# First conditioning in blocks of 512 columns, with a second ring of slots, in a diffusion backbone's inference step

## Chip, cores and metric

The kernel runs on one core of a Trainium2 chip. The metric is the device time of one execution in microseconds (us); it is lower when better. Engines are named as the profile names them: PE is TensorE (matmuls; PEld its weight loads), DVE is VectorE, ACT is ScalarE, POOL is GpSimd, SP is SyncE, which here only issues transfers.

## What is computed

Two layers of a backbone work on 128 context tokens and 256 latent tokens, 2048 wide. The part that matters is the start of a layer: the conditioning vectors (one for each of the two token groups) go through silu and the matrix w_ada, which gives six vectors; the first two, shift and scale, modulate the normalised tokens before the input projection.

```python
mods = jnp.split(jax.nn.silu(cvec) @ lp['w_ada'] + lp['b_ada'], 6, axis=-1)
sh1, sc1, g1, sh2, sc2, g2 = [m[:, None, :] for m in mods]
h = rms_norm(x, lp['g_pre1']) * (1.0 + sc1) + sh1
z = h @ lp['w_in']
...
x = x + g1 * rms_norm(mix, lp['g_post1'])
h = rms_norm(x, lp['g_pre2']) * (1.0 + sc2) + sh2
f = jnp.square(jax.nn.relu(h @ lp['w_mlp1'])) @ lp['w_mlp2']
x = x + g2 * rms_norm(f, lp['g_post2'])
```

w_ada is 2048 x 12288 per layer, in 32-bit floats. Nothing else of the layer can start before shift and scale of layer 0 are there: their 4096 columns (32 MB of weights) are the "first conditioning".

## The kernel before

Each engine has its own instruction stream, and semaphores order them. The first stage of layer 0, up to about 157 us, does four things beside each other.

Loads (SP, L371 to L376). SP first loads the conditioning vectors and x, and then, for each of eight pairs i, the weights of two blocks of 256 columns: block i (shift) and block 8 + i (scale). A block is four units of 512 rows x 256 columns, 512 KB each (`load_ada`, L342). The units go round a ring of four slots, `ada_raw`: SP waits on `ada_used` until the slot's last unit has been used by PE. Behind each pair comes one load of w_in (256 rows x 512 columns, `load_wide`, L335) into the ring `raw`, also of four slots. SP issues strictly in this order, so a waiting load holds back all loads behind it.

Conditioning (PE, `ada_unit`, L1462; `ada_turn`, L1473). For a unit PE does four matmuls of 256 columns with 32 columns of stationary data, each into its own quarter of the partitions of a bank of PSUM. When a block's four units are done, DVE copies the sums out (`ada_copy`, L829), PE turns and adds the quarters with two small matmuls, and DVE adds the bias and writes `mods` (`ada_mods`, L833). In PE's stream the turn of a block stands behind the second unit of the next block.

Rows (DVE, `first_rows`, L999; ACT, `h_high`, L563). With a pair's shift and scale the tiles 2i and 2i + 1 of the normalised, transposed x (in `full`) are modulated: DVE computes the coefficients, scales four pieces, ACT rounds the result to `h_hi`, and DVE subtracts for `h_lo`. Between the two DVE does `w_low` for a unit of w_in; ACT does `w_high` for it.

Projection (PE, `unit_rows`, L1535). The first four tiles of columns of the input projection are accumulated in banks 0 to 3 as rows become ready: one row unit is 24 matmuls of 384 columns, in four quarters of six. PE's order is written out by hand (L1547 to L1562): the quarters of row unit n/2 - 2 stand behind the units of even blocks n from 4 on; row units 6 and 7 stand after the last turn. x is turned into `full` (L1526) after the first three blocks; ACT counts the copies in `x_copied`. Afterwards ACT copies the four tiles to `z` (L558), and the next stage begins.

The memory of `z` is not in use in this stage but for `facc`, which holds x before it is turned.

Of the kernel before, what the change touches and what calls it, by code (L numbers as in the profile page):

```python
# [31 lines left out]
F32 = mybir.dt.float32  # L32
F32R = mybir.dt.float32r
ALU = mybir.AluOpType
# [3 lines left out]
P = 128  # L38
D = 2048
DEPTH = 2  # L40
CTX, LAT = 128, 256
TOK = CTX + LAT
# [71 lines left out]
PAIRS = 8  # L114
MOD = 256
# [47 lines left out]
def backbone(nc, x_prompt, x_sample, cache_k, cache_v, c, c_ctx, w_ada, b_ada, g_pre1, g_post1, g_pre2,  # L163
# [3 lines left out]
    with ctx:  # L167
        def sem(name):
            return ctx.enter_context(nc.semaphore(name))
# [7 lines left out]
        def at(name, shape, dt, offset):  # L177
            return nc.alloc_sbuf_tensor_at(name, [P, *shape], dt, offset=base + offset)
# [76 lines left out]
        junk = at("junk", [2, NC], F32, z_at + 4 * 16 * TOK)  # L255
        stats_at = z_at + 4 * (19 * TOK + 256)
# [19 lines left out]
        ada_landed = [sem(f"ada_landed{s}") for s in range(SLOTS)]  # L276
        hi_ready, lo_ready, unit_used, acc_free = sems("hi_ready lo_ready unit_used acc_free")
# [50 lines left out]
        def _(sp):  # L328
# [13 lines left out]
            def load_ada(layer, m, j, wait=True, n=None):  # L342

                n = m if n is None else n
                if wait:
                    sp.wait_ge(ada_used, 4 * n + j - 3)
                src = w_ada[layer, 512 * j:512 * j + 512, bass.ds(m * UC, UC)]
                sp.dma_start(ada_raw[:, j, :, :], src.rearrange("(k p) n -> p k n", p=P)).then_inc(ada_landed[j], 16)
# [467 lines left out]
        def _(dve):  # L816
# [12 lines left out]
            def ada_copy(n, bank=BANK_ADA):  # L829
                dve.wait_ge(ada_used, 4 * n + 4)  # L830
                nc.vector.tensor_copy(ada_s[:, :], ps[:, bank, 0:UC]).then_inc(ada_copied, 1)

            def ada_mods(layer, m, n, bank=BANK_ADA):  # L833
                dve.wait_ge(ada_turned, n + 1)
                nc.vector.tensor_tensor(mods[:, layer, bass.ds(m * 2, 2), :],
                                        ps[:, bank, MOD:MOD + 4].rearrange("p (t g) -> p t g", g=2),
                                        pb[:, layer, bass.ds(m * 2, 2)].unsqueeze(2).to_broadcast([P, 2, 2]),
                                        ALU.add).then_inc(mods_ready, 1)
# [160 lines left out]
            def first_rows(i):  # L999

                kts = slice(2 * i, 2 * i + 2)
                if i == 0:
                    dve.wait_ge(x_copied, 12)
                dve.wait_ge(mods_ready, 2 * i + 2)
                chain.link(nc.vector.scalar_tensor_tensor(
                    out=coef[:, 0, kts, :], in0=mods[:, 0, SC1 + 2 * i:SC1 + 2 * i + 2, :], scalar=1.0,
                    in1=pa[:, 0, G_PRE1 + 2 * i:G_PRE1 + 2 * i + 2].unsqueeze(2).to_broadcast([P, 2, 2]), op0=ALU.add, op1=ALU.mult))
                for kt in (2 * i, 2 * i + 1):
# [3 lines left out]
                last.then_inc(full_ready, 1)  # L1012
                w_low(i % 4, i // 4)
                dve.wait_ge(h_hi_ready, i + 1)
                nc.vector.tensor_tensor(h_lo[:, kts, :], full[:, kts, :], h_hi[:, kts, :].bitcast(F32),
                                        ALU.subtract).then_inc(h_ready, 1)

            for i in range(PAIRS):
                ada_copy(2 * i, ADA_FIRST[0])
                ada_mods(0, i, 2 * i, ADA_FIRST[0])  # L1020
                if i:
                    first_rows(i - 1)
                ada_copy(2 * i + 1, ADA_FIRST[1])
                ada_mods(0, PAIRS + i, 2 * i + 1, ADA_FIRST[1])
            first_rows(PAIRS - 1)

            for layer in range(DEPTH):
# [227 lines left out]
                def ada_products(lo, i, b, j, mark0):  # L1255
# [3 lines left out]
                    dve.wait_ge(ada_landed[j], 16 * (n + 1))  # L1259
# [104 lines left out]
        def _(pe):  # L1364
# [97 lines left out]
            def ada_unit(n, j, bank=BANK_ADA, read=None):  # L1462

                read = n if read is None else read
                pe.wait_ge(ada_landed[j], 16 * (n + 1))
                if j == 0 and not (isinstance(read, int) and read <= 0):
                    pe.wait_ge(mods_ready, read)
                for g in range(4):
                    last = nc.tensor.matmul(ps[32 * g:32 * g + 32, bank, 0:UC], cond[:, 4 * j + g, :], ada_raw[:, j, g, :],  # L1469
                                            start=j == 0, stop=j == 3)  # L1470
                last.then_inc(ada_used, 1)

            def ada_turn(n, bank=BANK_ADA, read=None):  # L1473

                read = n if read is None else read
                pe.wait_ge(ada_copied, n + 1)
                if not (isinstance(read, int) and read <= 0):
                    pe.wait_ge(mods_ready, read)
                for t in range(2):
                    last = nc.tensor.matmul(ps[:, bank, MOD + 2 * t:MOD + 2 * t + 2], ada_s[:, P * t:P * t + P], sel[:, :],  # L1480
                                            start=True, stop=True)
                last.then_inc(ada_turned, 1)

# [63 lines left out]
            for n in range(2 * PAIRS):  # L1547
                for j in range(4):
                    ada_unit(n, j, ADA_FIRST[n % 2], n - 1)
                    if j == 1 and n:  # L1550
                        ada_turn(n - 1, ADA_FIRST[(n - 1) % 2], n - 2)
                    if n >= 4 and n % 2 == 0:
                        unit_rows(n // 2 - 2, j)
                if n == 0:
                    turn_rows()
                if n < 3:
                    for g in range(4 * n, 4 * n + 4):
                        turn_first_x(g)
            ada_turn(2 * PAIRS - 1, ADA_FIRST[1], 2 * PAIRS - 2)
# [264 lines left out]
```

## Time and profile before

| what | us |
|---|---|
| median of 3 runs | 3325.29 |
| lowest, highest run | 3323.32, 3329.78 |
| the profiled execution | 3325.19 |
| its span, first to last instruction | 3323.4 |
| PE busy in the span | 3197.0 |
| DVE busy | 2178.8 |
| ACT busy | 1118.7 |
| end of the first stage, from the span's start | 156.9 |

The profile is of one execution. Busy time is summed per engine; matmuls are pipelined and their ends are modelled, so a busy PE need not be at its peak. The chain of waits follows the work that ended last back from releaser to releaser. A window gives busy times, the granted clock of TensorE (1.00 is 2.4 GHz, 0.50 is 1.2 GHz), the share of time of the 16 DMA engines, and what they moved.

### The profile page before, as it was taken

How to read it: one execution, taken by the hardware profiler on the slowest of the kernel's cores; microseconds unless marked ns; L12 is line 12 of the kernel's file. 1: busy time of each engine (PE TensorE's matmuls, PEld its weight loads, DVE VectorE, ACT ScalarE, POOL GpSimd, SP SyncE). 2: the span in 40 equal slices, each digit the busy share in tenths (PEclk: the TensorE clock that was granted, in tenths of full speed). 3: DMA queues.
4: the chain of work that ended last, by engine and by line, in shares of the span. 5: the costliest groups of instructions: out<-in, count | busy, mean ns of one | idle time of the engine just before them, and what ended most of it. 6: DMA issues, size and time to landing. Idle time of an engine off the chain costs nothing.

```text
span 3323.4 us, 48314 instructions
## 1 busy us (share of the span) xinstructions
PE 3197.0 (96%) x17401; PEld 2774.8 (83%) x17401; DVE 2178.8 (66%) x3132; ACT 1118.7 (34%) x1567; POOL 180.7 (5%) x211
## 2 busy tenths in 40 slices
PE   6899999999999999999998999999999999999999
PEld 3588755788998988989987996679899899898997
DVE  2357665598989889889896787667556463333335
ACT  2122333442333323323334334344233233332332
POOL 0001033000000000000000202300000000000000
PEclk8899999999999999999999999999999999999999
DMA  9866475266666676666662431125545444344342
GB/s 301 278 195 202 150 245 166 77 216 221 228 211 208 216 235 223 221 216 227 211 199 92 121 125 56 64 76 178 171 138 174 157 151 127 127 127 129 129 127 102
DMA packets 420022, 566.40 MB, mean 170 GB/s; under 512 B 17688, under 2 KB 276368, under 8 KB 419504
## 3 DMA queue, kind: packets, MB, share of 16 engines
q1 hardware_dynamic: 417600, 560.02, 52.3%
q0 software_dynamic: 1344, 4.33, 0.4%
q8 instruction: 76, 1.25, 0.2%
q14 instruction: 58, 0.48, 0.0%
q10 hardware_dynamic: 944, 0.32, 0.0%
HBM read 560.93 MB, written 3.67 MB: 170 GB/s over the span
## 4 chain that ended last, share of the span: by engine, by line
PE 85%; DVE 7%; issue 3%; ACT 3%; DMA 2%; SPq 0%; DVEq 0%; ACTq 0%
PE ps L1371 41%; PE ps L1379 34%; PE ps L1469 2%; DMA ada_raw<-in_w_ada_dram 2%; DVE ada_sums L1272 1%; PE ps L1542 1%; DVE w_lo L826 1%; PE ps L1653 1%; PE ps L1627 1%; DVE conv L1057 1%; PE ps L1641 1%; PE ps L1400 1%; ACT facc L584 1%; ACT w_hi L544 1%; PE ps L1614 1%
## 5 line engine op out<-in xcount | busy, mean ns | idle before, releaser
L826 DVE TENSOR_TENSOR w_lo<-raw,w_hi 128x1024 fp32r<-128x1024 f32 x672 | 825.9, 1233 | 767.3 <-ACT w_hi L544 741.3
L544 ACT ACTIVATE w_hi<-raw 128x1024 fp32r<-128x1024 f32 x672 | 710.8, 1058 | 1480.5 <-PE ps L1379 780.7
L1371 PE MATMUL ps<-h_hi,w_hi 128*128 128x384 f32 x2752 | 929.8, 338 | 8.0 <-DVE w_lo L826 7.0
L1371 PE MATMUL ps<-h_hi,w_lo 128*128 128x384 f32 x2752 | 923.1, 335 | 0.0
L1371 PE MATMUL ps<-h_lo,w_hi 128*128 128x384 f32 x2752 | 923.1, 335 | 0.0
L1379 PE MATMUL ps<-w_hi,hid_hi 128*128 128x512 f32 x1536 | 600.7, 391 | 2.6 <-DVE facc L1292 2.6
L1379 PE MATMUL ps<-w_hi,hid_lo 128*128 128x512 f32 x1536 | 598.1, 389 | 0.0
L1379 PE MATMUL ps<-w_lo,hid_hi 128*128 128x512 f32 x1536 | 598.1, 389 | 0.0
L1272 DVE SCALAR_TENSOR_TENSOR ada_sums<-ada_raw,cond,ada_sums 128x512 f32<-128x512 f32 x840 | 575.3, 746 | 0.0
L1371 PEld LDWEIGHTS ps<-h_hi,w_hi 128*128 128x128 f32 x2752 | 519.1, 189 | 25.0 <-issue 11.5
L1371 PEld LDWEIGHTS ps<-h_lo,w_hi 128*128 128x128 f32 x2752 | 519.2, 189 | 1.1
L1371 PEld LDWEIGHTS ps<-h_hi,w_lo 128*128 128x128 f32 x2752 | 519.2, 189 | 0.0
L1379 PEld LDWEIGHTS ps<-w_hi,hid_hi 128*128 128x128 f32 x1536 | 288.3, 188 | 64.4 <-DVE facc L1292 5.5
L1379 PEld LDWEIGHTS ps<-w_lo,hid_hi 128*128 128x128 f32 x1536 | 288.3, 188 | 60.2
L1379 PEld LDWEIGHTS ps<-w_hi,hid_lo 128*128 128x128 f32 x1536 | 288.3, 188 | 58.9
L1379 PE MATMUL ps<-w_hi,h_hi 128*128 128x512 f32 x384 | 162.6, 423 | 0.0
L1379 PE MATMUL ps<-w_lo,h_hi 128*128 128x512 f32 x384 | 151.6, 395 | 0.0
L1379 PE MATMUL ps<-w_hi,h_lo 128*128 128x512 f32 x384 | 151.5, 395 | 0.0
L1469 PE MATMUL ps<-ada_raw,cond 128*32 128x256 f32 x1280 | 105.9, 417 | 46.1 <-DMA ada_raw<-in_w_ada_dram 39.3
L1057 DVE SCALAR_TENSOR_TENSOR conv<-glu,pc,conv 128x384 f32<-128x384 f32 x240 | 141.9, 653 | 0.0
L1292 DVE TENSOR_TENSOR facc<-facc,ps 128x512 f32<-128x512 f32 x168 | 115.1, 685 | 30.4 <-PE ps L1379 28.5
L781 ACT ACTIVATE z<-ps 128x768 f32<-128x768 f32 x64 | 52.2, 815 | 202.8 <-PE ps L1371 202.8
(192 smaller groups left out, 2054.9 us busy)
## 6 DMA issues: line engine op xcount, KB each, us to landing
raw<-in_w_mlp_dram SPq DMA_DIRECT2D x512, 512.0 KB, 4.0
ada_raw<-in_w_ada_dram SPq DMA_DIRECT2D x384, 512.0 KB, 4.6
raw<-in_w_in_dram SPq DMA_DIRECT2D x96, 512.0 KB, 4.6
raw<-in_w_out_dram SPq DMA_DIRECT2D x64, 512.0 KB, 3.6
out_dram<-x SPq DMA_DIRECT2D x6, 512.0 KB, 2.6
x<-in_x_sample_dram SPq DMA_DIRECT2D x1, 2048.0 KB, 10.3
pw_w<-in_w_conv_pw_dram POOLq DMA_DIRECT2D x2, 1024.0 KB, 8.3
x<-in_x_prompt_dram SPq DMA_DIRECT2D x1, 1024.0 KB, 5.0
```

The source lines that it names most:

```text
L544: nc.scalar.activation(w_hi[:, j % 4, :, :], raw[:, j % 4, :, :], ACT.Copy).then_inc(hi_ready, 1)
L584: nc.scalar.activation(facc[:, place(n), t, :], x[:, t, NC * n:NC * n + NC], ACT.Square, accum_out=ss_x[:, t, n:n + 1]).then_inc(x_squared, 1)
L781: nc.scalar.activation(z[:, 16:18, :], ps[:, 2 * pair:2 * pair + 2, 0:TOK], ACT.Relu).then_inc(acc_free, 1)
L826: nc.vector.tensor_tensor(w_lo[:, j % 4, :, :], raw[:, j % 4, :, :], w_hi[:, j % 4, :, :].bitcast(F32), ALU.subtract).then_inc(lo_ready, 1)
L1057: op = nc.vector.scalar_tensor_tensor(out=out, in0=src, scalar=w, in1=out, op0=ALU.mult, op1=ALU.add)
L1272: op = nc.vector.scalar_tensor_tensor(out=out, in0=src, scalar=by, in1=out, op0=ALU.mult, op1=ALU.add)
L1292: nc.vector.tensor_tensor(dst, dst, ps[:, BANK_ACC + t, :], ALU.add).then_inc(acc_added, 1)
L1371: last = nc.tensor.matmul(ps[:, 2 * pair + t, 0:TOK], w[:, j % 4, k, P * t:P * t + P], v[:, kt + k, :], start=begin and k == 0 and i == 0, ...
L1379: last = nc.tensor.matmul(ps[:, BANK_ACC + t, :], v[:, kt + k, tokens(t)], wide(w, j)[:, k, :], start=begin and k == 0 and i == 0, stop=en ...
L1400: last = nc.tensor.matmul(ps[:, 2 * (n % 2) + g, P * i:P * i + P], coef[:, k, 4 * n + i, g:g + 1].to_broadcast([P, P]), ident[:, :], start ...
L1469: last = nc.tensor.matmul(ps[32 * g:32 * g + 32, bank, 0:UC], cond[:, 4 * j + g, :], ada_raw[:, j, g, :], start=j == 0, stop=j == 3)
L1542: last = nc.tensor.matmul(ps[:, t, 0:TOK], wide(w, u)[:, k, P * t:P * t + P], v[:, 2 * u + k, :], start=u == 0 and k == 0 and i == 0, stop ...
```

## The change

The sixteen blocks of 256 columns of the first conditioning become eight blocks of 512 columns, in the order shift, scale, shift, scale and so on; a block is eight units of 256 rows x 512 columns (still 512 KB). A unit is two matmuls of 512 columns; even units go into the first two quarters of the partitions, odd ones into the last two. Units 4 to 7 of the blocks from 2 on go to a second ring of four slots, `ada_aside`, which lies in the memory of `z` where `facc` was; before its first load SP waits for the last copy of x. A block's sums are copied in two halves to `ada_row`, turned with four small matmuls and added in two halves. `first_rows` works on four tiles at once, with `w_low` of its first unit ahead of the wait for the scale. A load of w_in follows the fourth unit of each block. Row units start with block 3; row unit 5 stands around the last turn, 6 and 7 behind it.

```diff
+ADA_FIRST_BLOCKS = 8
+ADA_ASIDE = ADA_FIRST_BLOCKS - 2
...
+        ada_aside = at("ada_aside", [SLOTS, 4, UC], F32, z_at)
+        ada_row = at("ada_row", [NC], F32, z_at + 4 * 20 * TOK)
...
-            for i in range(PAIRS):
-                for h, m in enumerate((i, PAIRS + i)):
-                    for j in range(4):
-                        load_ada(0, m, j, wait=2 * i + h > 0, n=2 * i + h)
-                load_wide(i % 4, i // 4, w_in, 0, 2 * P * i, CA0 * P, wait=i >= 4)
+            for n in range(ADA_FIRST_BLOCKS):
+                for u in range(8):
+                    aside = n >= 2 and u >= 4
+                    if n <= 2 and not aside:
+                        if 8 * n + u >= 4:
+                            sp.wait_ge(ada_used, 8 * n + u - 3)
+                    elif n == 2:
+                        sp.wait_ge(x_copied, 12)
+                    else:
+                        sp.wait_ge(ada_used, 8 * (n - 1) + u + 1)
+                    col = D * (n % 2) + NC * (n // 2)
+                    src = w_ada[0, 2 * P * u:2 * P * u + 2 * P, col:col + NC].rearrange("(k p) n -> p k n", p=P)
+                    sp.dma_start(wide(ada_aside if aside else ada_raw, u), src).then_inc((aside_landed if aside else ada_landed)[u % 4], 16)
+                    if u == 3:
+                        load_wide(n % 4, n // 4, w_in, 0, 2 * P * n, CA0 * P, wait=n >= 4)
...
+            def rows_copy(n):
+                dve.wait_ge(ada_used, 8 * n + 8)
+                for b in range(2):
+                    nc.vector.tensor_copy(ada_row[:, UC * b:UC * b + UC],
+                                          ps[:, ADA_FIRST[n % 2], UC * b:UC * b + UC]).then_inc(ada_copied, 1)
+            def rows_mods(n):
+                tile = DT * (n % 2) + 4 * (n // 2)
+                dve.wait_ge(ada_turned, 2 * n + 2)
+                for b in range(2):
+                    kts = slice(tile + 2 * b, tile + 2 * b + 2)
+                    nc.vector.tensor_tensor(mods[:, 0, kts, :],
+                                            ps[:, ADA_FIRST[n % 2], 4 * b:4 * b + 4].rearrange("p (t g) -> p t g", g=2),
+                                            pb[:, 0, kts].unsqueeze(2).to_broadcast([P, 2, 2]), ALU.add).then_inc(mods_ready, 1)
+            def first_rows(c):
+                quad_kts = slice(4 * c, 4 * c + 4)
+                if c == 0:
                     dve.wait_ge(x_copied, 12)
+                w_low(2 * c % 4, c // 2)
+                dve.wait_ge(mods_ready, 4 * c + 4)
...
+                for kt in range(4 * c, 4 * c + 4):
                     for g, a, b in GROUPS:
                         last = nc.vector.tensor_scalar(full[:, kt, a:b], full[:, kt, a:b], coef[:, 0, kt, g:g + 1],
                                                        mods[:, 0, SH1 + kt, g:g + 1], ALU.mult, ALU.add)
+                    if kt % 2:
+                        last.then_inc(full_ready, 1)
+                for i in (2 * c, 2 * c + 1):
+                    kts = slice(2 * i, 2 * i + 2)
+                    if i % 2:
+                        w_low(i % 4, i // 4)
+                    dve.wait_ge(h_hi_ready, i + 1)
+                    nc.vector.tensor_tensor(h_lo[:, kts, :], full[:, kts, :], h_hi[:, kts, :].bitcast(F32),
+                                            ALU.subtract).then_inc(h_ready, 1)
+            for n in range(ADA_FIRST_BLOCKS):
+                rows_copy(n)
+                rows_mods(n)
+                if n % 2:
+                    first_rows(n // 2)
...
+            def rows_unit(n, u):
+                if n >= 2 and u >= 4:
+                    pe.wait_ge(aside_landed[u % 4], 16 * (n - 1))
+                else:
+                    pe.wait_ge(ada_landed[u % 4], 16 * (2 * n + u // 4 + 1 if n < 2 else n + 3))
+                if n >= 2 and u == 0:
+                    pe.wait_ge(mods_ready, 2 * (n - 1))
+                for k in range(2):
+                    g = 2 * (u % 2) + k
+                    last = nc.tensor.matmul(ps[32 * g:32 * g + 32, ADA_FIRST[n % 2], :], cond[:, 2 * u + k, :],
+                                            wide(ada_aside if n >= 2 and u >= 4 else ada_raw, u)[:, k, :], start=u < 2, stop=u >= 6)
+                last.then_inc(ada_used, 1)
+            def rows_turn(n):
+                for b in range(2):
+                    pe.wait_ge(ada_copied, 2 * n + 2)
+                    for t in (2 * b, 2 * b + 1):
+                        last = nc.tensor.matmul(ps[:, ADA_FIRST[n % 2], 2 * t:2 * t + 2], ada_row[:, P * t:P * t + P], sel[:, :],
+                                                start=True, stop=True)
+                    last.then_inc(ada_turned, 1)
...
+            for n in range(ADA_FIRST_BLOCKS):
+                for u in range(8):
+                    rows_unit(n, u)
+                    if u == 1 and n:
+                        rows_turn(n - 1)
+                    if n >= 3 and u % 2 == 0:
+                        unit_rows(n - 3, u // 2)
+                    if u % 4 == 3 and 2 * n + u // 4 < 3:
+                        if n == 0 and u == 3:
+                            turn_rows()
+                        for g in range(4 * (2 * n + u // 4), 4 * (2 * n + u // 4) + 4):
+                            turn_first_x(g)
+            unit_rows(ADA_FIRST_BLOCKS - 3, 0)
+            unit_rows(ADA_FIRST_BLOCKS - 3, 1)
+            rows_turn(ADA_FIRST_BLOCKS - 1)
+            unit_rows(ADA_FIRST_BLOCKS - 3, 2)
+            unit_rows(ADA_FIRST_BLOCKS - 3, 3)
             for u in range(PAIRS - 2, PAIRS):
                 for part in range(4):
                     unit_rows(u, part)
```

Lines of the old forms of these functions, and the counts of loads in later waits (less six, which went to the other ring), are left out.

## Rows read from the trace of the kernel before

**Rows 1.** The page's first part: busy us, share of the span, instructions.

```profile
PE 3197.0 (96%) x17401; PEld 2774.8 (83%) x17401; DVE 2178.8 (66%) x3132; ACT 1118.7 (34%) x1567; POOL 180.7 (5%) x211
```

**Rows 2.** Chain of waits, 0 to 260 us: shares by line; pieces (start, us, what).

```profile
by line: PE ps L1371 22.4%; DMA ada_raw<-in_w_ada_dram 22.3%; PE ps L1542 18.2%; PE ps L1469 13.5%; DMA raw<-in_w_in_dram 5.3%; DVE conv L1057 3.5%; DVE w_lo L826 3.4%; PE ps L1480 3.0%; PE ps L1532 2.4%; ACT w_hi L544 1.2%; SPq L348 1.1%; 
...
54.67 6.01 DMA ada_raw<-in_w_ada_dram
...
123.08 6.29 DMA ada_raw<-in_w_ada_dram
```

**Rows 3.** Waits, 44 to 140 us: who waited for whom, us, times, longest.

```profile
SPq L348 <- PE ps L1469: 75.1, 39, 4.1
...
PE ps L1469 <- DMA ada_raw<-in_w_ada_dram: 23.0, 11, 3.4
```

**Rows 4.** Windows: us, each engine's busy time (instructions), granted clock, DMA share, GB/s.

```profile
0.00:20.00 20.00, 3.44 (x25) 0.81 (x25) 2.39 (x12) 8.68 (x10) 2.27 (x13) 1.00 0.89 305
20.00:44.00 24.00, 19.42 (x174) 12.06 (x170) 8.16 (x24) 8.80 (x15) 0.00 (x0) 0.93 0.95 316
...
60.00:140.00 80.00, 62.55 (x459) 37.20 (x460) 18.21 (x46) 7.96 (x9) 0.00 (x0) 0.77 0.86 275
...
62.00:64.00 2.00, 2.00 (x10) 1.56 (x12) 0.00 (x0) 0.00 (x0) 0.00 (x0) 0.50 1.09 365
...
82.00:88.00 6.00, 6.00 (x45) 3.60 (x44) 0.59 (x2) 0.00 (x0) 0.00 (x0) 0.91 0.67 215
...
146.00:151.00 5.00, 5.00 (x16) 5.00 (x17) 4.63 (x9) 3.65 (x4) 1.13 (x2) 0.50 1.10 353
...
896.00:904.00 8.00, 8.00 (x37) 6.62 (x36) 4.41 (x7) 2.12 (x2) 0.00 (x0) 1.00 1.05 394
```

**Rows 5.** PE's groups by shape, 53.9 to 54.95 us: busy us, mean ns, idle.

```profile
L1469 PE MATMUL ps<-ada_raw,cond 128*32 128x256 f32 x16 | 1.1, 385 | 0.0
```

**Rows 6.** Chain of waits, single pieces of PE: start, us, line, instructions.

```profile
25.71 1.00 PE ps L1469 x16
...
50.39 0.57 PE ps L1469 x8
50.96 1.25 PE ps L1542 x6
...
61.81 2.22 PE ps L1542 x6
64.03 1.01 PE ps L1469 x8
...
140.38 0.55 PE ps L1480 x4
```

**Rows 7.** Timeline, 0 to 160 us: start, us, engine, line, operation, tiles, count.

```profile
38.47 2.00 ACT L662 ACTIVATE full<-ps 128x512 f32<-128x512 f32 x3 [0.26 <-PE ps L1532]
...
41.31 1.07 PE L1469 MATMUL ps<-ada_raw,cond 128*32 128x256 f32 x16
...
142.60 0.64 PE L1469 MATMUL ps<-ada_raw,cond 128*32 128x256 f32 x8 [1.00 <-DMA ada_raw<-in_w_ada_dram]
...
146.31 1.25 DVE L1010 TENSOR_SCALAR full<-full,coef,mods 128x128 f32<-128x128 f32 x4
...
147.59 0.84 ACT L565 ACTIVATE h_hi<-full 128x768 fp32r<-128x768 f32 x1 [0.79 <-DVE full L1010]
```

**Rows 8.** Chain of waits, end of the first stage: start, us, line, instructions.

```profile
145.88 11.01 PE ps L1542 x48
156.91 0.82 ACT z L558
```

**Rows 9.** DVE's groups by line, 60 to 140 us: busy us, mean ns, idle.

```profile
L826 DVE TENSOR_TENSOR w_lo<-raw,w_hi 128x1024 fp32r<-128x1024 f32 x4 | 4.9, 1218 | 0.0
L1015 DVE TENSOR_TENSOR h_lo<-full,h_hi 128x768 fp32r<-128x768 f32 x4 | 3.8, 952 | 0.0
L831 DVE COPY ada_s<-ps 128x256 f32<-128x256 f32 x9 | 3.8, 422 | 18.7 <-PE ps L1469 18.7
```

More of the change, by code:

```diff
@@ L276, in backbone @@
         ada_landed = [sem(f"ada_landed{s}") for s in range(SLOTS)]
+        aside_landed = [sem(f"aside_landed{s}") for s in range(SLOTS)]
         hi_ready, lo_ready, unit_used, acc_free = sems("hi_ready lo_ready unit_used acc_free")
@@ L340, in load_wide, with load_ada @@
                 sp.dma_start(wide(raw, j), src).then_inc(raw_landed[j % 4], 16)
[L342 to L346, printed above, removed]
+            def load_ada(layer, m, j):
+                sp.wait_ge(ada_used, 4 * m + j - 3)
                 src = w_ada[layer, 512 * j:512 * j + 512, bass.ds(m * UC, UC)]
@@ L827, in w_low, with ada_copy, ada_mods @@
                                         ALU.subtract).then_inc(lo_ready, 1)
-            def ada_copy(n, bank=BANK_ADA):
+            def ada_copy(n):
                 dve.wait_ge(ada_used, 4 * n + 4)
-                nc.vector.tensor_copy(ada_s[:, :], ps[:, bank, 0:UC]).then_inc(ada_copied, 1)
-            def ada_mods(layer, m, n, bank=BANK_ADA):
+                nc.vector.tensor_copy(ada_s[:, :], ps[:, BANK_ADA, 0:UC]).then_inc(ada_copied, 1)
+            def ada_mods(layer, m, n):
                 dve.wait_ge(ada_turned, n + 1)
                 nc.vector.tensor_tensor(mods[:, layer, bass.ds(m * 2, 2), :],
-                                        ps[:, bank, MOD:MOD + 4].rearrange("p (t g) -> p t g", g=2),
+                                        ps[:, BANK_ADA, MOD:MOD + 4].rearrange("p (t g) -> p t g", g=2),
                                         pb[:, layer, bass.ds(m * 2, 2)].unsqueeze(2).to_broadcast([P, 2, 2]),
@@ L998, in _ @@
             chain.link(nc.vector.tensor_scalar(nsinks[:, :, :], sinks[:, :, :], -1.0, None, ALU.mult))
-            def first_rows(i):
-                kts = slice(2 * i, 2 * i + 2)
-                if i == 0:
+            def rows_copy(n):
[14 more added lines that the diff above has]
+                if c == 0:
                     dve.wait_ge(x_copied, 12)
-                dve.wait_ge(mods_ready, 2 * i + 2)
+                w_low(2 * c % 4, c // 2)
+                dve.wait_ge(mods_ready, 4 * c + 4)
                 chain.link(nc.vector.scalar_tensor_tensor(
-                    out=coef[:, 0, kts, :], in0=mods[:, 0, SC1 + 2 * i:SC1 + 2 * i + 2, :], scalar=1.0,
-                    in1=pa[:, 0, G_PRE1 + 2 * i:G_PRE1 + 2 * i + 2].unsqueeze(2).to_broadcast([P, 2, 2]), op0=ALU.add, op1=ALU.mult))
-                for kt in (2 * i, 2 * i + 1):
+                    out=coef[:, 0, quad_kts, :], in0=mods[:, 0, SC1 + 4 * c:SC1 + 4 * c + 4, :], scalar=1.0,
+                    in1=pa[:, 0, G_PRE1 + 4 * c:G_PRE1 + 4 * c + 4].unsqueeze(2).to_broadcast([P, 4, 2]), op0=ALU.add, op1=ALU.mult))
+                for kt in range(4 * c, 4 * c + 4):
                     for g, a, b in GROUPS:
@@ L1011, in first_rows @@
                                                        mods[:, 0, SH1 + kt, g:g + 1], ALU.mult, ALU.add)
[L1012 to L1025, printed above, removed]
+                    if kt % 2:
[12 more added lines that the diff above has]
+                    first_rows(n // 2)
             for layer in range(DEPTH):
@@ L1258, in ada_products @@
                     begin = b % 2 == 0 and j == 0
-                    dve.wait_ge(ada_landed[j], 16 * (n + 1))
+                    dve.wait_ge(ada_landed[j], 16 * (n + 1 - ADA_ASIDE))
                     if begin:
@@ L1460, in h_wait, with ada_unit @@
                 pe.wait_ge(norm_lo, 12 * (p - 1) + 8 + j + 1)
[L1462 to L1467, printed above, removed]
+            def ada_unit(n, j):
+                pe.wait_ge(ada_landed[j], 16 * (n + 1 - ADA_ASIDE))
+                if j == 0:
+                    pe.wait_ge(mods_ready, n)
@@ L1468, in ada_unit, with ada_turn @@
                 for g in range(4):
-                    last = nc.tensor.matmul(ps[32 * g:32 * g + 32, bank, 0:UC], cond[:, 4 * j + g, :], ada_raw[:, j, g, :],
+                    last = nc.tensor.matmul(ps[32 * g:32 * g + 32, BANK_ADA, 0:UC], cond[:, 4 * j + g, :], ada_raw[:, j, g, :],
                                             start=j == 0, stop=j == 3)
                 last.then_inc(ada_used, 1)
-            def ada_turn(n, bank=BANK_ADA, read=None):
-                read = n if read is None else read
+            def ada_turn(n):
@@ L1476, in ada_turn @@
                 pe.wait_ge(ada_copied, n + 1)
-                if not (isinstance(read, int) and read <= 0):
-                    pe.wait_ge(mods_ready, read)
+                pe.wait_ge(mods_ready, n)
                 for t in range(2):
-                    last = nc.tensor.matmul(ps[:, bank, MOD + 2 * t:MOD + 2 * t + 2], ada_s[:, P * t:P * t + P], sel[:, :],
+                    last = nc.tensor.matmul(ps[:, BANK_ADA, MOD + 2 * t:MOD + 2 * t + 2], ada_s[:, P * t:P * t + P], sel[:, :],
                                             start=True, stop=True)
@@ L1545, in unit_rows @@
                     last.then_inc(unit_used, 1)
[L1547 to L1559, printed above, removed]
+            for n in range(ADA_FIRST_BLOCKS):
[15 more added lines that the diff above has]
+            unit_rows(ADA_FIRST_BLOCKS - 3, 3)
             for u in range(PAIRS - 2, PAIRS):
```

## Prediction

> **What bounds the kernel now.** I read the page's engine table first. TensorE is busy for 96% of the span [rows 1], so a change of the loads can only pay where TensorE is not the limit. The chain of waits cut to the first 260 us finds that place: 22.3% of it is "DMA ada_raw", weights of the first conditioning that have not landed [rows 2]. Five such pieces of 6.0 to 6.5 us stand in it, from 54.7 to 123.1 us, one for each pair of blocks [rows 2]. Behind the stage (it ends at 156.9 us, when the first columns of the input projection are copied out) the chain is mostly TensorE again, so what is won here should stay won.
>
> Why do the weights come late? The waits show both sides of one ring. From 44 to 140 us TensorE waits 23.0 us for ada_raw, while SP waits 75.1 us, 39 times, for TensorE to free one of the four slots before it may issue the next load [rows 3]. The windows show what this does to the DMA: over 60 to 140 us it moves 275 GB/s, but 365 in a stretch with loads queued (62 to 64 us) and 215 in one where SP waits (82 to 88 us) [rows 4]. Between two conditioning units TensorE runs a quarter of a row unit (six matmuls, L1542), and only then is the next slot freed. The ring is too shallow for that rhythm: the stage is limited by loads that could have been issued earlier. The same rows show a granted clock of 0.77 from 60 to 140 us: TensorE starts at half clock after each wait.
>
> **The loads.** All 72 loads of 512 KB (64 conditioning, 8 of w_in) remain; their rows grow from 1 KB to 2 KB, and from the second half of block 2 eight slots are in flight instead of four. A full queue gave 353 GB/s with 1 KB rows (146 to 151 us) and 394 with 2 KB rows in the MLP (896 to 904 us, conditioning loads of the very shape that the change introduces) [rows 4]. I take 390, with 355 as the lower bound. Until 44 us nothing is faster, since the first 20 conditioning units still go through four slots. Counting bytes from the windows (305 GB/s to 20 us is mostly x; 316 after it [rows 4]), I estimate some 19.5 loads landed by 44 us, and charge the new kernel one load for units that hold their slot longer: 18.5. The other 53.5 loads are 28.0 MB and need 71.9 us at 390 GB/s: the last lands at 116 us at the earliest. At 355 GB/s it is 123 us. One block (nine loads, 4.72 MB) takes 12.1 us at 390 and 13.3 at 355.
>
> The row of 394 GB/s [rows 4] speaks against a limit near 358. The Trainium skill (HBM Reference, "Specifications (TRN2)") gives about 358 GB/s per core when both cores of a memory domain stream, though the same page has one core alone above it. With 358 the 28.0 MB would last until 122.2 us and the stage end near 142, one to two us later than my sum. One core runs here, and the trace sides with the higher figure.
>
> **TensorE in a new block.** A unit is now two matmuls of 512 columns on two of the four column groups, instead of four of 256 on all four. That the groups run side by side is visible: 16 instructions of 385 ns mean fit in 1.1 us [rows 5]. One unit now costs 0.57 us at full clock and two in a row 1.00 [rows 6], so a unit streams 0.43 us and ends 0.14 later. The new unit streams twice as long: 0.86 + 0.14 = 1.00 us alone. Two consecutive units use different groups; the second can start when the first is at its second pass, which gives 3 x 0.43 + 0.14 = 1.43 us for a pair. No row shows that overlap; without it a pair costs 2 x 0.86 + 0.14 = 1.86. Units 7 and 0, 3 and 4, 5 and 6 are neighbours; 1 and 2 have the turn between them. A block is then 3 x 1.43 + 2 x 1.00 for units, 4 x 1.25 for the quarter units of rows [rows 6], and twice the old turn of 0.55 (1.1) [rows 6]: 12.4 us; without overlap 13.7. At half clock a quarter takes 2.22 and an old unit 1.01 [rows 6], so a whole block would take nearly twice as long, about 22.5 us. TensorE and the DMA thus come out level at 12.1 to 12.4 us. I take 13.0 per block: the floor plus some 0.6, for one start at half clock (about 4 us, spread over five blocks, is 0.8) and for the two not meshing exactly, less what the buffer hides.
>
> **Sum.** Block 3 can start when load 28 has landed: 9.5 loads after 44 us, 1.34 us each, at 57 us. Blocks 3 to 7 at 13.0 us end at 122 us. Before, the last conditioning unit ran at 142.6 us and ended at 143.2 [rows 7]: 21 us later.
>
> **The tail gets longer.** Before, from 143.2 to 156.9 us: 13.7 us, most of it two row units in 11.01 us, partly at half clock [rows 8]. After the change, three units remain. Behind the last conditioning unit TensorE first runs half of unit 5 (2 x 1.25 = 2.5 us), and the two copies of 0.42 [rows 9] hide under it; the turn ends at 3.6, the two additions of 8 columns, which are smaller than a copy (0.3 for both, an estimate), at 3.9. DVE then does w_low(6), which now stands ahead of the modulation (1.2 [rows 9]), the coefficients (smaller still, 0.1) and four of the eight scalings (1.25 [rows 7]): 6.5 us. The rounding on ACT takes 0.84 [rows 7] beside the other four scalings, which end at 7.7; h_lo adds 0.95 [rows 9]: 8.7 us. Units 6 and 7 follow, eight quarters at 1.25 at most: 18.7 us; at 1.1 each 17.5, with a half-clock start as before 19.7. I take 18.5. TensorE stands idle for some 2.5 us in it. Stage end: 122 + 18.5 = 140.5 instead of 156.9, a gain of 16.4 us.
>
> **Edits that I cost at nothing.** The new SP wait on x_copied: behind it in the queue stand all later loads, but the last copy of x ended at 40.5 us, and SP gets to that wait only after unit 15, which ran from 41.3 to 42.4 us [rows 7]; without that cover each us of lateness would be a us of the stage. The loads of w_in move half a block forward and wait for lo_ready as before; w_low(n-4) is by then more than a block old. DVE's work for two blocks (4 copies, 4 small additions, 8 scalings, 2 w_low, 2 h_lo: 1.7 + 0.6 + 2.5 + 2.4 + 1.9, about 9 us [rows 7, 9]) lies beside 26 us of TensorE; if a copy came more than 3 us late, the turn would hold TensorE by the rest. For the loads of the next stage SP waits for w_low(6) and w_low(7), some 5 and 10 us after the last unit, in the tail's shadow: the first is needed at 18.5.
>
> **Rivals.**
> First, TensorE takes the place of the DMA at a mixed clock. The windows grant 0.77 from 60 to 140 us [rows 4], that is, half clock for 46% of the time. If that share stays, a block of 12.4 us takes 12.4 / (0.54 + 0.46 x 0.55) = 15.6 us, five end at 135, the stage at 153.5, 3.4 us early: 3321.8 us. For it: with only two column groups in use the mix has less work per us than before. Against it: the low clock stood behind the waits of 6 us, which a ring twice as deep should remove.
> Second, slower: half clock throughout. The mechanism is the same place, the two-group units in blocks 3 to 7, but now busy TensorE never gets the full clock back. At 22.5 us a block the last unit ends at 170 and the stage at 190: 33 us later, 3358 us. It decides from a block of (156.9 - 18.5 - 57) / 5 = 16.3 us, where the gain is gone. For it: from 60.7 to 69 us TensorE ran without a gap and yet stayed at half clock; the quarter of 2.22 and the unit of 1.01 us are from there [rows 6]. Against it: at 50 to 54 us the same mix ran at full clock.
> Third, the change doesn't do what it says: the rate does not rise with the deeper queue and stays at the 275 GB/s of 60 to 140 us. The last load then lands at 44 + 28.0/0.275 = 146 us, and with the longer tail the stage ends at 165: 3333 us, slower by a little more than can be told. The 365 and 353 GB/s with queued loads [rows 4] speak against it.
> Better than the sum: both floors met exactly (12.4 a block, tail 17.5) give 119 + 17.5 = 136.5 us, 20 us early: 3305 us.
>
> **How the numbers follow.** The profiled execution took 3325.19 us, of which the span is 3323.4; the median of the runs shown is 3325.29, so both are the same reference. 3325.2 - 16.4 = 3308.8, rounded to 3309. Chances: forecast and its surroundings (3304 to 3316) 0.66, mixed clock 0.14, half clock 0.11, no higher rate 0.05, better than 3304 us 0.04. The forecast's own range: no overlap of units (13.7 a block plus a start at half clock, 14.5) and the tail of 19.7 give 129.5 + 19.7 = 149, so 3317; the floor gives 3305. The range to be held 8 times in 10 adds the mixed clock: 3302 to 3322 us. Faster by over 0.2% (6.7 us, about what can be told from no change): 0.66 + 0.04 + 0.03 of the mixed clock, 0.73. Within 0.2%: the rest of that, 0.11. Slower: 0.11 + 0.05 = 0.16.
>
> **What would show it.** Right: the window of 60 to 115 us shows over 340 GB/s and a clock over 0.9; the pieces "DMA ada_raw" of 6 us are gone from the chain, the last conditioning unit ends near 122 us and the first copy to z starts near 140. TensorE should be the longest entry of the chain in blocks 3 to 7, and a wait of 2 to 3 us on DVE should stand in the tail. Wrong: a clock of 0.8 or less with TensorE fully busy (first two rivals), SP still waiting with the DMA under 300 GB/s (third), a TensorE wait at the turn (DVE late), or a stage behind 140 us that is longer than before by what was won.

## The result, and the profile after

The changed kernel took 3300.69 us (median of 4 runs, 3294.59 to 3304.30), the kernel before beside it 3325.37: a ratio of 0.992, 95% interval 0.9908 to 0.9932, 24.7 us faster. The forecast of 3309 had the direction, and the mechanism with it; the time lies 1.3 us below its range of 3302 to 3322. The profiled execution is the fastest of the four (3294.59 us).

The page's engine table has hardly moved ([rows 1]; busy us, share of the span, instructions):

```profile
PE 3189.4 (97%) x17145; PEld 2754.8 (84%) x17145; DVE 2176.2 (66%) x3128; ACT 1117.5 (34%) x1567; POOL 180.8 (5%) x211
```

In this execution TensorE's busy time is 7.6 us shorter and the span (3292.8 us) 30.6 us shorter than before, so most of the gain is waiting. The stage that was changed shows it. These are windows of the kernel after (us, busy time of PE, PEld, DVE, ACT and POOL, granted clock, DMA share, GB/s):

```profile
20.00:44.00 24.00, 19.23 (x118) 8.50 (x118) 6.29 (x18) 7.47 (x13) 0.00 (x0) 1.00 0.97 344
44.00:60.00 16.00, 12.50 (x62) 4.26 (x60) 7.70 (x19) 3.47 (x4) 0.00 (x0) 1.00 1.04 381
60.00:115.00 55.00, 54.76 (x288) 27.04 (x284) 16.91 (x42) 6.95 (x8) 0.00 (x0) 1.00 1.05 386
```

Against [rows 4]: 386 GB/s where 275 were moved, a clock of 1.00 where 0.77 was granted, and TensorE busy for 54.76 of 55 us. Where the stage ends is read from the chain of waits, 0 to 260 us (start, us, what):

```profile
44.12 11.05 DMA ada_raw<-in_w_ada_dram
...
55.20 1.08 PE ps L1523 x4
...
56.30 11.82 DMA ada_raw<-in_w_ada_dram
...
68.17 1.05 PE ps L1523 x4
...
71.44 0.98 PE ps L1532 x8
...
74.65 1.34 PE ps L1523 x8
76.00 1.26 PE ps L1594 x6
77.25 1.45 PE ps L1523 x8
...
83.65 0.98 PE ps L1532 x8
...
95.81 0.98 PE ps L1532 x8
...
108.01 0.98 PE ps L1532 x8
...
116.51 0.98 PE ps L1523 x4
117.49 2.31 PE ps L1594 x12
119.80 0.80 PE ps L1532 x8
...
120.62 0.23 DVE mods L1025 x2
120.85 1.13 DVE w_lo L839
...
122.10 2.41 DVE full L1041 x8
124.50 0.88 DVE h_lo L1050
...
125.52 8.58 PE ps L1594 x48
...
134.12 0.82 ACT z L571
```

L1523 is a conditioning unit, L1532 the turn of a block, L1594 the rows of the projection. Block 3 starts at 55.20 us, block 4 at 68.17; the turns from 71.44 to 108.01 stand 12.2 us apart; the last unit ends at 117.49; the rest is the tail; the first copy to z starts at 134.12, where before it started at 156.91 [rows 8]. So the stage gives 22.8 us in this execution, against 24.7 between the medians. In this stage loads stand in the chain up to 68 us and not behind it; of the pieces of 6 us that came with each pair of blocks [rows 2] none is left. One row of the timeline (start, us, engine, line, operation, tiles, and in brackets the idle time before it and what ended it) has TensorE's wait in the tail, 2.75 us for DVE:

```profile
125.52 0.41 PE L1594 MATMUL ps<-h_hi,w_hi 128*128 128x384 f32 x1 [2.75 <-DVE h_lo L1050]
```

The waits from 68 to 116 us (who waited for whom, us, times, longest) say it less cleanly:

```profile
PEld ps L1523 <- DMA ada_aside<-in_w_ada_dram: 2.2, 8, 0.3
PEld ps L1523 <- DMA ada_raw<-in_w_ada_dram: 2.1, 4, 1.1
...
SPq L386 <- PE ps L1523: 23.0, 17, 2.2
```

TensorE's weight loads still wait for transfers, 4.3 us in four blocks, while SP waits for TensorE. Which of the two sets the 12.2 us? The chain alone says TensorE. The experiments below say otherwise.

### The profile page after: what moved, and what is told of

It reads as the page before. It is cut to its first block, busy times and chain, and to the rows that moved or that the text cites. A ratio compares the mean times of both kernels' runs of the same rounds, so it can differ in the third digit from the quotient of the medians.

```text
span 3292.8 us, 47782 instructions
## 1 busy us (share of the span) xinstructions
PE 3189.4 (97%) x17145; PEld 2754.8 (84%) x17145; DVE 2176.2 (66%) x3128; ACT 1117.5 (34%) x1567; POOL 180.8 (5%) x211
## 4 chain that ended last, share of the span: by engine, by line
PE 84%; DVE 7%; issue 3%; ACT 3%; DMA 2%; SPq 0%; DVEq 0%; ACTq 0%
PE ps L1403 41%; PE ps L1411 35%; DVE ada_sums L1304 1%; DMA ada_raw<-in_w_ada_dram 1%; PE ps L1500 1%; DVE w_lo L839 1%; PE ps L1523 1%; PE ps L1709 1%; DVE conv L1089 1%; PE ps L1594 1%; PE ps L1683 1%; DMA raw<-in_w_in_dram 1%; PE ps L1697 1%; PE ps L1432 1%; ACT w_hi L557 1%
## 5 line engine op out<-in xcount | busy, mean ns | idle before, releaser
L1411 PEld LDWEIGHTS ps<-w_hi,h_hi 128*128 128x128 f32 x384 | 73.0, 190 | 37.5 <-issue 21.0
```

The costliest lines, as they stand in the source:

```text
L1411: last = nc.tensor.matmul(ps[:, BANK_ACC + t, :], v[:, kt + k, tokens(t)], wide(w, j)[:, k, :], start=begin and k == 0 and i == 0, stop=en ...
```

## Experiments

**Which part of the change brings it?** First the wide rows without the second ring.

```diff
-ADA_ASIDE = ADA_FIRST_BLOCKS - 2
+ADA_ASIDE = 0
...
-                    aside = n >= 2 and u >= 4
-                    if n <= 2 and not aside:
-                        if 8 * n + u >= 4:
-                            sp.wait_ge(ada_used, 8 * n + u - 3)
...
+                    aside = False
+                    if 8 * n + u >= 4:
+                        sp.wait_ge(ada_used, 8 * n + u - 3)
...
```

> The changed kernel with the second ring taken out: blocks of 512 columns go round the one ring of four slots all the time; everything else as in the changed kernel. The first stage ended at 156.9 us before and at 134.1 after the change. If the depth of the ring brings the gain, the DMA falls back below 300 GB/s from 60 us on, TensorE waits for ada_raw again, the granted clock of the stage is below 0.9 and the stage ends at 150 to 160 us (total 3318 to 3328). If the wider rows of 2 KB bring it, the rate stays over 350 and the stage ends at 136 to 142 us (total 3302 to 3310).

Measured: 3314.64 us, ratio 0.9969 (0.9956 to 0.9981), stage end 145.68: between the two forecasts, and so is the rate. Its window of 60 to 115 us, columns as above:

```profile
60.00:115.00 55.00, 51.42 (x247) 23.85 (x247) 16.93 (x42) 6.95 (x8) 0.00 (x0) 0.97 0.95 329
```

And two of the seven loads that stand in its chain from 57 to 122 us:

```profile
71.53 6.98 DMA ada_raw<-in_w_ada_dram
...
101.41 6.50 DMA ada_raw<-in_w_ada_dram
```

Then the second ring without the wide rows: the kernel before, its blocks of 256 columns, with four more slots in the same memory.

```diff
+ADA_ASIDE = 6
...
+        ada_aside = at("ada_aside", [SLOTS, 4, UC], F32, z_at)
...
+                        aside = n >= 5 and n % 2 == 1
+                        if n == 5:
+                            sp.wait_ge(x_copied, 12)
+                        elif n >= 6:
+                            sp.wait_ge(ada_used, 4 * (n - 2) + j + 1)
...
```

> The kernel before with the second ring alone: blocks of 256 columns, rows of 1 KB, the old order of PE and DVE, but the odd blocks from the fifth on go to a second ring of four slots in the memory of z. If depth brings the gain, loads come at the 355 GB/s that a full queue gave with 1 KB rows: 28 MB after 44 us last until 123 us, and with the old tail of 13.7 us the stage ends near 138 us (total near 3306). If the wider rows bring it, the stage ends above 150 us.

Measured: 3307.38 us, ratio 0.9955 (0.9939 to 0.9972), stage end 141.75, where depth alone was to give 138. The same window of this kernel:

```profile
60.00:115.00 55.00, 46.15 (x392) 28.54 (x384) 18.33 (x47) 7.40 (x9) 0.00 (x0) 0.91 1.09 352
```

And of the kernel before, for comparison:

```profile
60.00:115.00 55.00, 41.77 (x300) 24.75 (x301) 13.21 (x33) 6.06 (x7) 0.00 (x0) 0.75 0.87 282
```

The blocks of 512 with four slots end the stage 11.2 us earlier, depth alone 15.2, both 22.8. They share a cause (a load that lands late), so their gains don't add up. With eight slots of 1 KB rows the DMA engines are busy throughout (share 1.09) at 352 GB/s; with four slots they are not (0.87 and 0.95). Depth fills the queue, width raises what a full queue moves.

The first of the two runs is not the wide rows alone: it keeps the new order too, in which TensorE's row work stands behind every second unit of each block and not in the even blocks only. By share of busy time the loads went from 282 / 0.87 = 324 to 329 / 0.95 = 346 GB/s, and the share itself from 0.87 to 0.95. The higher share may come from the order; no run here separates order and width in four slots. The run with the deep ring and 256 columns keeps the old order, and in it TensorE waits 4.3 us between 60 and 116 us for DVE's h_lo, so its 7.6 us behind the whole change need not be the width alone.

**Was it the clock?** Before, a quarter of a row unit took 2.22 us behind a wait of 6 us, and 1.25 at full clock [rows 6]. Filler matmuls into a free bank, whose sums nobody reads, keep it at work in the kernel before: seven to a pair of blocks, then only three.

```diff
+                    if n == 4 and j == 0:
+                        pe.wait_ge(x_copied, 12)
+                    if n >= 5 and n % 2 == 1 and j >= 2:
+                        keep_warm(2, X_BANKS[0])
+                    if n >= 6 and n % 2 == 0 and j == 0:
+                        keep_warm(3, X_BANKS[0])
                     ada_unit(n, j, ADA_FIRST[n % 2], n - 1)
```

> The kernel before with filler matmuls (identity, 512 columns, into a bank that is not in use) in TensorE's waits of blocks 5 to 14: two ahead of the third and the fourth unit of each odd block, three ahead of the next even block. They add some 6 us of work for each pair of blocks at most, in a wait of about the same size, and should hold the clock at full. If the half clock is what made the stage slow, it ends at 140 to 147 us. If the shallow ring is, the loads still come at under 300 GB/s, and the stage ends between 150 and 158 us although the clock is near 1.0.

Measured: 3327.78 us, ratio 1.0008 (0.9999 to 1.0018), stage end 156.00. Its window:

```profile
60.00:115.00 55.00, 55.00 (x347) 27.45 (x345) 14.12 (x35) 6.76 (x7) 0.00 (x0) 1.00 0.88 283
```

Inconclusive: the clock is full, but the fillers fill TensorE to the brim (55.00 of 55 us), so the loads wait for the fillers instead of for the slow clock. Hence the lighter dose:

```diff
+                    if n == 4 and j == 0:
+                        pe.wait_ge(x_copied, 12)
+                    if n >= 5 and (n % 2 == 1 and j >= 2 or n % 2 == 0 and j == 0):
+                        keep_warm(1, X_BANKS[0])
```

> The kernel before with one filler matmul (0.85 us) at each place where the heavier version had two or three: ahead of the third and the fourth unit of each odd block from the fifth on and ahead of the next even block. TensorE's own work per pair of blocks is then 10.6 + 2.6 = 13.2 us, well under the 16.7 us that a pair took, so the fillers cannot set the pace as they may have in the heavier version. If the half clock made the stage slow, it ends below 147 us; if the ring of four did, at 152 to 158 us, with the clock at 0.9 or more and under 300 GB/s.

Measured: 3313.84 us, ratio 0.9966 (0.9954 to 0.9979), stage end 149.19, between the two forecasts. Its window:

```profile
60.00:115.00 55.00, 47.67 (x344) 25.21 (x348) 13.86 (x35) 6.75 (x7) 0.00 (x0) 0.97 0.92 296
```

At a clock of 0.97 the old ring moves 296 GB/s, far from 386, and the stage ends 7.7 us earlier. So the half clock cost the old stage 7.7 us or somewhat more, on the loads and in the tail together, since the fillers keep TensorE busy for 1.1 us each; what is left of the 22.8, some 15 us at most, needs the ring or the blocks of 512. A deeper ring brings most of the clock along by itself (0.91 with 256 columns, from 0.75 before).

**What sets the 12.2 us of a block?** I had put TensorE's floor at 12.4 us, with a pair of neighbouring units at 1.43 us; the chain shows pairs of 1.34 to 1.46. The first of three tests puts neighbours on the same column groups, so that they can't overlap.

```diff
-                    g = 2 * (u % 2) + k
+                    g = 2 * (u % 4 in (1, 2)) + k
```

> The changed kernel with another choice of column groups: units 0, 3, 4 and 7 use the first two, 1, 2, 5 and 6 the last two, so that neighbours (7 and 0, 3 and 4, 5 and 6) share groups and cannot run side by side. The sums are the same. If TensorE is the limit and the overlap of neighbours is real, a pair of units grows from 1.45 to about 1.86 us, a block from 12.4 to 13.7, and the stage ends near 140.6 us instead of 134.1. If the DMA is the limit, it ends within 1 us of 134.1.

Measured: 3309.40 us, ratio 0.9952 (0.9936 to 0.9969), stage end 143.25, 9.1 us later than after (2.3 of it stand ahead of block 3, and 1.6 is half clock in the last 48 matmuls, 10.19 us). Its chain:

```profile
87.74 0.98 PE ps L1532 x8
...
90.95 1.84 PE ps L1523 x8
...
101.19 0.98 PE ps L1532 x8
```

A pair costs 1.84 us (1.86 was worked out for no overlap) and turns stand 13.45 us apart. Now TensorE is the bound: from 68 to 116 us it waits for no load. The overlap is real, and worth 1.25 us in each block of the changed kernel. Which engine bounds the changed kernel itself this run can't say, though its end is nearer to the forecast for TensorE: without the overlap TensorE's block is longer than the 12.2 us of the changed kernel in any case.

The second test halves every load from block 3 on, so that the DMA can't be the bound.

```diff
-                    src = w_ada[0, 2 * P * u:2 * P * u + 2 * P, col:col + NC].rearrange("(k p) n -> p k n", p=P)
+                    size = NC if n < 3 else NC // 2
+                    src = w_ada[0, 2 * P * u:2 * P * u + 2 * P, col:col + size].rearrange("(k p) n -> p k n", p=P)
...
```

> The changed kernel with half of each conditioning load from block 3 on: only the first 256 of a unit's 512 columns are fetched, the other half of the slot keeps old data (so the shift and scale are wrong there), and the matmuls stay. After the change blocks 3 to 7 took 62.2 us, 12.4 each. If TensorE is what limits them, the stage still ends at 133 to 135 us, at some 220 GB/s. If the DMA does, it ends at 128 us or earlier.

Measured: 3295.51 us in one run, stage end 130.40, although its last 48 matmuls took 10.17 us where those of after took 8.58. Its chain:

```profile
92.46 0.98 PE ps L1533 x8
...
95.67 1.00 PE ps L1524 x8
...
103.45 0.98 PE ps L1533 x8
```

And one pair in its timeline (start, us, engine, line, operation, tiles, count):

```profile
95.60 0.62 PE L1524 MATMUL ps<-ada_raw,cond 128*32 128x512 f32 x2
95.61 0.62 PE L1524 MATMUL ps<-ada_aside,cond 128*32 128x512 f32 x2
...
96.05 0.60 PE L1524 MATMUL ps<-ada_raw,cond 128*32 128x512 f32 x2
96.07 0.60 PE L1524 MATMUL ps<-ada_aside,cond 128*32 128x512 f32 x2
```

This decides it. Turns stand 11.0 us apart: TensorE's floor is 11.0 us, not 12.4. Once both neighbours' data are there they start 0.01 us apart, and the pair costs 1.00 us, as much as one unit alone (0.98). In the changed kernel the second neighbour starts 0.36 us behind the first, and its weight load (PEld) waits for a transfer:

```profile
74.58 0.62 PE L1523 MATMUL ps<-ada_raw,cond 128*32 128x512 f32 x2
74.94 0.14 PEld L1523 LDWEIGHTS ps<-ada_aside,cond 128*32 128x32 f32 x4 [0.22 <-DMA ada_aside<-in_w_ada_dram]
```

Three pairs at 1.00 in place of 1.42 are the whole of the difference of 1.2 us. The end lay between those of both theories: the DMA was the bound, but by 1.2 us a block and no more.

The third test takes work from TensorE instead: two of three products of row units 1 to 4 are left out.

```diff
                     for i, (w, v) in enumerate(((w_hi, h_hi), (w_hi, h_lo), (w_lo, h_hi))):
+                        if 0 < u < 5 and i < 2:
+                            continue
```

> The changed kernel with a third of the products of row units 1 to 4: of the three products of each only the last is left (the projection's sums are wrong), which takes two thirds of the row work out of blocks 4 to 7. A quarter falls from 1.25 to some 0.55 us and TensorE's work in such a block from 12.4 to 9.6 us. If the DMA is level with TensorE, as its 387 GB/s say (12.2 us for nine loads), the stage ends no earlier than 132 us. If the loads have room to spare, it ends near 134.1 - 4 x 2.8 = 123 us.

Measured: 3307.68 us in one run, stage end 136.54, of which 1.6 is the half clock in its last 48 matmuls (10.14 us). Its window:

```profile
60.00:115.00 55.00, 50.44 (x229) 17.20 (x231) 17.14 (x44) 6.94 (x8) 0.00 (x0) 1.00 1.05 387
```

And its chain, two of the four pieces of this length:

```profile
67.07 11.39 DMA ada_aside<-in_w_ada_dram
...
91.79 11.76 DMA ada_aside<-in_w_ada_dram
```

Less work gains nothing: loads move into the chain, at the same 387 GB/s. Both tests agree that in the changed kernel the DMA sets the pace.

**The tail and the front.** Two edits follow from the readings above. In the tail DVE's 1.13 us of w_low stand between the additions to `mods` and the scalings, while TensorE will soon be idle: w_low goes ahead of rows_mods, where TensorE still works, and one quarter of unit 5 instead of two stands ahead of the last turn.

```diff
-                w_low(2 * c % 4, c // 2)
                 dve.wait_ge(mods_ready, 4 * c + 4)
...
+                if n % 2:
+                    w_low(n // 2 * 2 % 4, n // 4)
                 rows_mods(n)
...
             unit_rows(ADA_FIRST_BLOCKS - 3, 0)
-            unit_rows(ADA_FIRST_BLOCKS - 3, 1)
             rows_turn(ADA_FIRST_BLOCKS - 1)
+            unit_rows(ADA_FIRST_BLOCKS - 3, 1)
```

> The changed kernel with two moves in the tail: w_low of a group's first row unit stands between the copy and the additions of the second block, where DVE waits for the turn (2.3 us in the last block), instead of behind the additions; and one quarter of row unit 5 instead of two stands ahead of the last turn. The last unit ended at 117.5 us and the stage at 134.1. If the tail is the chain that I read (turn, w_low, modulation, rounding, h_lo, then 48 matmuls), each move takes off 1.1 to 1.2 us and the stage ends near 131.9 us. If TensorE's own work sets the tail, nothing moves. In the total 2.2 us is at the edge of what the runs can tell.

Measured: 3301.29 us, ratio 0.9921 (0.9907 to 0.9935). Its chain:

```profile
117.93 1.27 PE ps L1595 x6
...
123.91 8.58 PE ps L1595 x48
...
132.51 0.82 ACT z L571
```

The tail is 14.6 us long instead of 16.6 (2.0 us shorter, 2.2 were expected), but the total is no lower than that of after. The changed kernel itself, run again beside it, shows why:

> The changed kernel once more, unchanged, beside the shorter tail. If what is missing from the sum over the first stage (22.8 us of it in the profiled execution, 24.7 in the medians) is half-clock stretches behind the stage that fall differently from run to run, this median lies anywhere from 3297 to 3305 us, and the span behind the stage less half of its time at half clock is the 3145 us of the other kernels, within 2 us.

Measured: 3303.89 us, ratio 0.9932 (0.9918 to 0.9946), stage end 136.02. Span and mean clock of the first profile of after:

```profile
core 0: 3292.8 us, clock 0.993
```

The same of this one:

```profile
core 0: 3302.0 us, clock 0.989
```

And its last 48 matmuls in the chain, 1.6 us longer at a partly low clock:

```profile
125.84 10.16 PE ps L1594 x48
```

The same program differs by 9.2 us between two executions, 1.9 of them in this stage and 7.3 behind it. An estimate from windows of 5 us behind the stage (TensorE's busy time, times what the granted clock lacks to 1.00) gives 17.1 us lost to half clock in the first profile, 26.1 in the repeat and 21.7 in the kernel before; without it the rest takes 3141.6, 3139.9 and 3144.8 us. So the clock makes the difference between the two executions, as was thought, though by this estimate the repeat misses the expected 3145 by 5 us. Single microseconds of this stage are therefore judged by its end, not by the total.

Last, the front. From 20 to 44 us the changed kernel still goes round four slots, at 344 GB/s. A third set of slots for units 4 to 7 of blocks 0 and 1, in memory of h_lo that is written only later, gives eight from the start, on top of the shorter tail:

```diff
+        ada_early = at("ada_early", [SLOTS, 4, UC], F32, lo_at + 4 * (DT * TOK - SLOTS * 4 * UC))
...
-                    if n <= 2 and not aside:
-                        if 8 * n + u >= 4:
-                            sp.wait_ge(ada_used, 8 * n + u - 3)
-                    elif n == 2:
+                    if n == 2 and u >= 4:
                         sp.wait_ge(x_copied, 12)
-                    else:
+                    elif n:
                         sp.wait_ge(ada_used, 8 * (n - 1) + u + 1)
+                    ring, landed = ((ada_raw, ada_landed) if u < 4 else (ada_early, early_landed) if n < 2 else (ada_aside, aside_landed))
...
```

> The kernel with the shorter tail (its stage ended at 132.51 us), and a third set of four slots that serves units 4 to 7 of blocks 0 and 1, so that eight loads are in flight from the start and not from the second half of block 2. Theory: the ring of four slots still sets the rate of the front; 20 to 44 us moved 344 GB/s where the full queue moves 387. At 387 that stretch would bring 24 x 43 / 387 = 2.7 us more of loads, so from 20 to 44 us I expect over 375 GB/s, the last conditioning unit about 2.7 us earlier (near 115), the stage end at 129 to 130.5 us, and the time 2 to 3 us below that of the short tail, 3297 to 3300, within the scatter of some 5 us that lies behind the stage. Rival: the front is set by x, its turns and its copies on TensorE and ACT, or the loads of x go through the same DMA engines and only the order changes; then the rate to 44 us stays near 345 and the stage ends at 132 to 133 us.

Measured: 3296.90 us, ratio 0.9908 (0.9892 to 0.9925). The window of the front:

```profile
20.00:44.00 24.00, 20.29 (x130) 9.28 (x130) 7.49 (x20) 7.45 (x13) 0.00 (x0) 1.00 1.05 385
```

And the end of the stage in its chain:

```profile
113.78 0.98 PE ps L1527 x4
...
129.34 0.82 ACT z L571
```

385 GB/s, the last unit done 3.2 us earlier than in the kernel with the short tail, the stage end at 129.34: as the theory said, and 4.8 us ahead of the changed kernel. It is the best version seen. By the totals alone it can't be told for certain from the changed kernel, since the intervals overlap (0.9892 to 0.9925 and 0.9908 to 0.9932), though its four runs (up to 3297.14 us) lie below all five of the repeat (from 3300.76).

## What the prediction had right, and the step that failed

**Right: the bound and the mechanism.** The ring held up loads that could have been issued, a fuller queue with wider rows moves more, and the clock comes back with it. Four slots or narrow rows alone stop at 329 and 352 GB/s; fillers without a ring at 296. The first two rivals, at a mixed or a half clock, fell with the clock of 1.00; the third, no higher rate, with 386 GB/s, close to the 390 that I took from [rows 4]. The edits costed at nothing cost nothing: no turn held TensorE, and the next stage began right behind the tail.

By the Trainium skill's 358 GB/s per core (HBM Reference, "Specifications (TRN2)"; meant for both cores of a domain) the estimate would have been 13.2 us for a block's nine loads of 4.72 MB. The trace gives 386 GB/s over 55 us and 12.2 us; one core runs here, and the measurement decides.

**Failed: the size of three terms,** all to the same side, the blocks most of all. The stage was to end at 140.5 us and ended at 134.1.

| term | predicted | measured | difference |
|---|---|---|---|
| start of block 3 | 57 | 55.2 | -1.8 |
| blocks 3 to 7 | 5 x 13.0 = 65.0 | 62.3 | -2.7 |
| tail | 18.5 | 16.6 | -1.9 |

The start: I charged one load for units that hold their slot longer and let the rate rise at 44 us; the windows show 344 GB/s where there were 316 from 20 to 44 us, with four slots in both, so the new blocks pay there already. The repeat agrees (54.85).

The blocks: the step that failed is the 13.0 us of a block, "the floor plus some 0.6". Block 3 did take 13.0 us, but the four behind it 12.3 each (68.17 to 117.49). The floor of 12.4 us was TensorE's, from a pair of 1.43 us that no row showed; it is 11.0, since neighbours on different column groups run fully side by side. So there were not two floors to mesh, but one, the DMA's 12.1 to 12.2 us, and next to nothing to add to it behind block 3. In the repeat the five blocks took 63.0. The pair of 1.34 to 1.46 us in the trace after would have confirmed the 1.43 to anyone who only looked there; it is a wait for the second neighbour's load inside a piece that the chain gives to TensorE.

The tail: I had 8.7 us up to units 6 and 7, with TensorE idle for 2.5 of it, and it took 8.0 with 2.75; then 9.8 for the eight quarters, and they took 8.58 at full clock. This term isn't fixed: in the repeat the same 48 matmuls took 10.16 us and the tail 18.2, close to the 18.5. The short tail of the first profile is in part luck with the clock.

With these three the sum would have been 3325.2 - 22.8 = 3302.4. The remaining 1.7 us to the median of 3300.69 lie within what executions of the same kernel differ by behind the stage. The spans less the stage show it: 3323.4 - 156.9 = 3166.5 us before, 3292.8 - 134.1 = 3158.7 in the first profile of after, 3302.0 - 136.0 = 3166.0 in the repeat. The first profile of after is the shortest of all twelve that were taken here (the others have 3163 to 3171). The repeat's median of 3303.89 lies inside the range, so that the first one lay outside is partly chance; that the start and the blocks were charged too much is not, since both executions show it. What decides where the low clock falls behind the stage, I didn't find out.

Last, the range: its lower end of 3302 took "both floors met exactly" (3305) as nearly the best that could be, with 0.04 below 3304. That best case held the unseen pair at 1.43 us. For the low end of the range a bound that no row shows should have been taken at its far end, full overlap: 1.00 for a pair, 11.1 for TensorE, and so 12.1 for a block by the DMA. With the start at 57 and the tail of 17.5 that gives 135.0 and 3303.3, and with the better start 3301.5: still above 3300.69, so the range also had to leave a few microseconds for executions that differ.

## What to carry to other kernels

Where an engine waits for loads while the queue waits for the engine, count the slots: here depth filled the queue and wide rows raised what a full queue moves, and either alone left part of the gain behind (15.2 us with depth, 11.2 with the blocks of 512 and their order, of 22.8). When two engines look level in a chain that one of them fills, take work from each in turn: halving the loads showed the floor of one (11.0 us), leaving out matmuls that of the other (12.2 us). Judge an edit of a few microseconds by the end of its own stage, and look whether the clock was the same there, where executions of one kernel differ by more than it is worth.

## What the runs showed of the hardware that I had not expected

- Two units of two matmuls each, with different weights and on different column groups, start 0.01 us apart and take 1.00 us together; one alone takes 0.98, and two on the same groups 1.84.
- Loads with 2 KB rows ran at 386 GB/s for 55 us; with 1 KB rows and as many slots the DMA engines were as busy (share 1.09 against 1.05) at 352.
- The mean clock of one program differed between two executions (0.993 and 0.989) and its span by 9.2 us, with no change in the code.
